# Odd layer's norm scale computed as columns and spread by a diagonal, and its first two input tiles multiplied side by side

## What is computed

```python
h_lat = rms_norm(x, norm_g[l]) * (1.0 + sc[:, None]) + sh[:, None]
h_ctx = rms_norm(ctx, norm_g[l]) * (1.0 + scc) + shc
# odd_mixer, pre(h), for context and column-ordered latents
xm, zg = jnp.split(h @ w_in, [ML_WIDTH], axis=-1)        # 2048 + 2048 columns
xcv = jax.nn.silu(centred_dwconv(xm, conv_w, conv_b))    # 4 taps along the tokens
# q, k, v and the gates g come from xcv and xm; zg gates the output
```

## Time and profile before

| | us |
|---|---|
| median of 3 runs | 3034.0 |
| the profiled execution | 3031.98 |
| its span, first to last instruction | 3030.3 |
| mean granted TensorE clock, share of full speed | 0.941 |
| DVE busy | 1542.8 |
| ACT busy | 843.1 |
| POOL busy | 1017.0 |

### The profile page before, as it was taken

One profiled execution on the slowest core, in us unless ns is written; L12 is line 12 of the kernel. 1 busy time (PEld: TensorE's weight loads), 2 busy tenths in 40 slices (PEclk: granted clock), 3 DMA queues, 4 the chain that ended last, 5 costly groups with the idle time before them and its releaser, 6 DMA issues.

```text
span 3030.3 us, 38093 instructions
## 1 busy us (share of the span) xinstructions
PE 2748.6 (91%) x13429; PEld 2132.5 (70%) x13429; DVE 1542.8 (51%) x2331; ACT 843.1 (28%) x1004; POOL 1017.0 (34%) x1181
## 2 busy tenths in 40 slices
PE   7994677998998999898996899998999999999898
PEld 5652665544444677887885677776788888888787
DVE  2204885487787322343324644577545555545711
ACT  1210454246256111322212322221323323231310
POOL 0000997788760000002123333343442423332000
PEclk8797888999999999899997999999999999999999
DMA  4520222010111666634113222245513131213521
GB/s 154 170 75 29 69 83 88 28 49 24 45 46 28 200 185 191 204 91 175 39 32 81 70 106 97 97 156 192 185 42 102 55 115 56 96 58 119 165 83 51
DMA packets 258720, 297.89 MB, mean 98 GB/s; under 512 B 34944, under 2 KB 222632, under 8 KB 258224
## 3 DMA queue, kind: packets, MB, share of 16 engines
q1 hardware_dynamic: 203104, 206.75, 21.6%
q10 hardware_dynamic: 50672, 72.89, 6.6%
q0 software_dynamic: 4832, 16.78, 1.9%
HBM read 203.09 MB, written 93.29 MB: 98 GB/s over the span
## 4 chain that ended last, share of the span: by engine, by line
PE 63%; DVE 10%; issue 4%; ACT 3%; POOL 1%; DMA 1%; DVEq 0%; SPq 0%; ACTq 0%; POOLq 0%
PE ps L130 55%; PE ps L1175 5%; PE ps L1024 1%; PE ps L1018 1%; DVE s_scan_tmp L1910 1%; DVE arena L1912 1%; DVE s_scan_tmp L1908 1%; DVE arena L485 1%; DVE xc_part L2204 1%; DVE arena L1961 0%; ACT arena L1337 0%; POOL h_part L2542 0%; ACT L1337 0%; DVE arena L1930 0%; PE ps L1180 0%
## 5 line engine op out<-in xcount | busy, mean ns | idle before, releaser
L130 PE MATMUL ps<-arena,weights 128*128 128x512 f32 (+2 forms) x2432 | 752.4, 488 | 52.4 <-ACT arena L1337 19.7
L130 PEld LDWEIGHTS ps<-arena,weights 128*128 128x128 f32 (+1 forms) x2432 | 398.5, 177 | 396.8 <-issue 325.0
L130 PE MATMUL ps<-h_part,in_weight_parts 128*128 128x512 f32 (+1 forms) x1920 | 420.6, 380 | 37.7 <-POOL in_weight_parts L2534 13.6
L130 PEld LDWEIGHTS ps<-h_part,in_weight_parts 128*128 128x128 f32 x1920 | 343.3, 192 | 110.5 <-POOL in_weight_parts L2534 14.3
L130 PE MATMUL ps<-v_part,p_part 128*128 128x512 f32 x1248 | 295.0, 395 | 0.1
L130 PEld LDWEIGHTS ps<-v_part,p_part 128*128 128x128 f32 x1248 | 234.2, 190 | 49.2 <-issue 0.9
L130 PE MATMUL ps<-q_part,xc_part 128*128 128x256 f32 x1920 | 249.0, 289 | 14.7 <-DVE v_part L2204 10.7
L130 PEld LDWEIGHTS ps<-q_part,xc_part 128*128 128x128 f32 x1920 | 238.5, 195 | 16.4 <-DVE v_part L2204 11.5
L1175 PE MATMUL ps<-wo_part,mx_part 128*128 128x512 f32 x768 | 183.8, 400 | 6.8 <-DVE mx_part L2204 6.2
L2531 POOL TENSOR_TENSOR in_weight_parts<-weights,ones 128x1024 fp32r<-128x1024 f32 x32 | 79.5, 2483 | 306.5 <-issue 213.7
L1175 PEld LDWEIGHTS ps<-wo_part,mx_part 128*128 128x128 f32 x768 | 145.6, 191 | 41.0 <-issue 6.4
(11 more groups left out here) (354 smaller groups left out, 4180.6 us busy)
## 6 DMA issues: line engine op xcount, KB each, us to landing
weights<-in_e_w_in SPq DMA_DIRECT2D x32, 512.0 KB, 4.2
weights<-in_o_w_in SPq DMA_DIRECT2D x32, 512.0 KB, 4.2
s_out_maps<-arena ACTq DMA_DIRECT2D x16, 640.0 KB, 2.9
weights<-in_mod_w POOLq DMA_DIRECT2D x20, 512.0 KB, 4.8
arena<-s_out_maps SPq DMA_DIRECT2D x16, 640.0 KB, 4.3
ml_xcv<-arena ACTq DMA_DIRECT2D x16, 640.0 KB, 3.0
xc_full<-ml_xcv SPq DMA_DIRECT2D x4, 2560.0 KB, 9.7
xm_tiles<-ml_xm SPq DMA_DIRECT2D x16, 640.0 KB, 3.9
```

Of the source, the lines that this page charges most:

```text
L130: return nc.tensor.matmul(o, lhsT, rhs, start=(k == 0), stop=(k == n - 1))
```

## The change

The sum over features is taken with the squares as weights and one column of ones as the moving side: ten products, one for each block of 128 tokens, leave the 1280 sums as ten columns of 128 partitions in bank 3. Root and reciprocal then work on 128 x 10. DVE multiplies the identity by these columns into ten diagonal blocks (diag, 128 x 1280), and PE multiplies them by ones: the scale of all tokens appears on all partitions, context in bank 6, latents in banks 4 and 5. ACT copies the context's scale to SBUF (rrow); DVE reads the latents' scale from PSUM. DVE makes all eight low parts; the unrounded copy h_full, ACT's second rounding and POOL's subtractions are gone. norm_tmp of k waits for the low part of k-2.

SP issues the first two weight loads ahead of the store of X2. PE runs tiles 0 and 1 together, k by k, into banks 0 to 2 and 3, 6, 7; ACT takes tile 0 out with two copies and tile 1 with four, one behind the other; the gate accumulation is opened after both. Then come tile 2, the sums of tiles 0 and 1, and the loop from tile 3. POOL's weight splits run one tile further ahead.

```diff
+        rsc, rrow = at(43584, NBLK), at(43600, CTX)
+        diag = at(43968, TOK).rearrange("p (b c) -> p b c", c=P)
+        psP = [[ps3[0][:, t0:t0 + n] for t0, n in SEGS], [ps[:, b, 0:n] for b, (t0, n) in zip((3, 6, 7), SEGS)]]
-        HL = over("h_full", DT * TOK, AR0 + 4 * XTo, F32)[:, :].rearrange("p (k t) -> p k t", k=DT)
...
             sp.wait_ge(*past("eo_wl", MT))
+            for s in range(2):
+                sp.dma_start(Wv[:, s], ow_in[s]).then_inc(sem(f"xz_w{s}"), 16)
             for s in range(2):
                 sp.wait_ge(*past(f"eo_ev{s}", 16))
             sp.dma_start(x2_d.rearrange("k p t -> p k t"), X2[:, :, CTX:TOK]).then_inc(sem("x_spilled"), 16)
...
-            with sp.Fori(0, MT // 2) as i:
+            with sp.Fori(1, MT // 2) as i:
                 for s in range(2):
                     input_weight(i, s)
...
             pe.wait_ge(*past("sq_total", 1))
-            for j, (t0, n) in enumerate(SEGS):
-                last = mm(ps[:, 4 + j, 0:n], ones[:, :], sq[1][:, 0, t0:t0 + n], 0, 1)
+            for b in range(NBLK):
+                last = mm(ps[:, 3, b:b + 1], sq[1][:, DT - 1, P * b:P * b + P], ones[:, 0:1], 0, 1)
             last.then_inc(sem("ss_mm1"), 1)
-            pe.wait_ge(*past("rms1", 3))
+            pe.wait_ge(*past("diag_ready", 1))
+            for b, (o, n) in ((0, (ps[:, 6, 0:CTX], 2)), (2, (ps[:, 4], 4)), (6, (ps[:, 5], 4))):
+                last = mm(o, ones[:, :], diag[:, b:b + n].rearrange("p b c -> p (b c)"), 0, 1)
+            last.then_inc(sem("scale_mm"), 1)
+            pe.wait_ge(*past("rms1", 1))
+            pe.wait_ge(*past("scale_row", 1))
+            for s in range(2):
+                pe.wait_ge(*past(f"xz_split{s}", 1))
+            for k in range(DT):
+                pe.wait_ge(*past("ht1_low", k + 1))
+                for s in range(2):
+                    for q, (a, b) in enumerate(PARTS):
+                        for j, (t0, n) in enumerate(SEGS):
+                            last = mm(psP[s][j], WXs[s][:, a, k], HTs[b][:, k, t0:t0 + n], 3 * k + q, 3 * DT)
+                    if k == DT - 1:
+                        last.then_inc(sem(f"xz_mm{s}"), 1)
+            pe.wait_ge(*past("xm_ev", 2))
             pe.wait_ge(*past("wf_zero", 1))
...
-            mixer_input(0, 0)
-            with pe.Fori(0, MT // 2 - 1) as i:
+            mixer_input(1, 0)
+            for s in range(2):
+                gate_sums(0, s)
+            with pe.Fori(1, MT // 2 - 1) as i:
                 mixer_input(i, 1)
                 gate_sums(i, 0)
                 mixer_input(i + 1, 0)
...
+                    nc.scalar.activation(rsc, ps[:, 3, 0:NBLK], ACT.Sqrt, bias=cols[:, 0:1], scale=1.0 / D).then_inc(sem("rms1"), 1)
+                    act.wait_ge(*past("scale_mm", 1))
+                    nc.scalar.activation(rrow, ps[:, 6, 0:CTX], ACT.Copy).then_inc(sem("scale_row"), 1)
...
-                    if l == 1 and k % 2:
-                        act.wait_ge(*past("ht1_full", k + 1))
-                        last = nc.scalar.activation(HTs[0][:, k], HL[:, k], ACT.Copy)
...
+            act.wait_ge(*past("xz_mm0", 1))
+            nc.scalar.activation(xmp[:, 0, 1:1 + CTX], psP[0][0][:, 0:CTX], ACT.Copy)
+            nc.scalar.activation(xmp[:, 0, LOFF + 1:LOFF + 1 + LAT], ps3[0][:, CTX:TOK], ACT.Copy).then_inc(sem("xm_ev"), 1)
+            act.wait_ge(*past("xz_mm1", 1))
+            nc.scalar.activation(xmp[:, 1, 1:1 + CTX], psP[1][0][:, 0:CTX], ACT.Copy)
+            x = LOFF + 1
+            for src in (psP[1][0][:, CTX:BANK], psP[1][1], psP[1][2]):
+                last = nc.scalar.activation(xmp[:, 1, x:x + src.shape[1]], src, ACT.Copy)
+                x += src.shape[1]
+            last.then_inc(sem("xm_ev"), 1)
+            for s in range(2):
+                mixer_rows(s, s)
+            with act.Fori(1, MT // 2) as i:
...
+                    link(V.reciprocal(rsc, rsc))
+                    V.tensor_tensor(diag, ident[:, :].unsqueeze(1).to_broadcast([P, NBLK, P]), rsc.unsqueeze(2).to_broadcast([P, NBLK, P]), ALU.mult).then_inc(sem("diag_ready"), 1)
+                    dve.wait_ge(*past("scale_mm", 1))
+                    dve.wait_ge(*past("scale_row", 1))
+                    scale = [psf[:, 4 * BANK:4 * BANK + LAT], rrow]
                 for k in range(DT):
...
-                    elif k >= 2 and k % 2:
-                        dve.wait_ge(*past("ht1_full", k - 1))
                     elif k >= 2:
-                        dve.wait_ge(*past("ht1_low", k // 2))
+                        dve.wait_ge(*past("ht1_low", k - 1))
...
-                    if l == 1 and k % 2:
+                    if l == 1 and k:
                         low_part(k - 1)
+                if l == 1:
+                    low_part(DT - 1)
...
                 input_weight(0, s)
-            for k in range(1, DT, 2):
-                pool.wait_ge(*past("ht1_high", k + 1))
-                pool.wait_ge(*past("bm", 3))
-                GP.tensor_tensor(HTs[1][:, k], HL[:, k], HTs[0][:, k].bitcast(F32), ALU.subtract).then_inc(sem("ht1_pool"), 1)
+            input_weight(1, 0)
             pool.wait_ge(*past("gates_open", 2))
             pool.wait_ge(*past("gates_mm", 1))
...
-                    input_weight(i + 1, s)
-            for m in range(2, MT):
+                    input_weight(i + (s + 1), 1 - s)
+            for m in range(3, MT):
                 input_weight((MT + m) // 2, m % 2)
```

More of the change, by code:

```diff
@@ L64 @@
 C_MCW = 256
-LATE_SIGNALS = ("sums", "ht1_full", "ht1_high", "ht1_low", "w_high", "xz_split0", "xz_split1", "xz_mm0", "xz_mm1",
+LATE_SIGNALS = ("sums", "scale_mm", "ht1_high", "ht1_low", "w_high", "xz_split0", "xz_split1", "xz_mm0", "xz_mm1",
     "xc_in", "xm_in0", "xm_in1", "xr_stored", "xb_in", "zt_in", "out_stored0", "out_stored1",
@@ L987, in mixer_input @@
                 for k in range(DT):
-                    if k % 2:
-                        pe.wait_ge(*past("ht1_pool", k // 2 + 1))
-                    else:
-                        pe.wait_ge(*past("ht1_low", k // 2 + 1))
                     for q, (a, b) in enumerate(PARTS):
@@ L1218, in norm @@
                 act.wait_ge(*past(f"ss_mm{l}", (DT, 1)[l]))
-                for j, (t0, n) in enumerate(SEGS):
-                    nc.scalar.activation(rstd[l][:, t0:t0 + n], ps[:, 4 + j, 0:n], ACT.Sqrt, bias=cols[:, 0:1], scale=1.0 / D).then_inc(sem(f"rms{l}"), 1)
+                if l == 0:
+                    for j, (t0, n) in enumerate(SEGS):
+                        nc.scalar.activation(rstd[0][:, t0:t0 + n], ps[:, 4 + j, 0:n], ACT.Sqrt, bias=cols[:, 0:1], scale=1.0 / D).then_inc(sem("rms0"), 1)
+                else:
+                    nc.scalar.activation(rsc, ps[:, 3, 0:NBLK], ACT.Sqrt, bias=cols[:, 0:1], scale=1.0 / D).then_inc(sem("rms1"), 1)
+                    act.wait_ge(*past("scale_mm", 1))
+                    nc.scalar.activation(rrow, ps[:, 6, 0:CTX], ACT.Copy).then_inc(sem("scale_row"), 1)
                 for k in range(DT):
@@ L1488, in _, with mixer_rows @@
             norm(1)
-            with act.Fori(0, MT // 2) as i:
+            def mixer_rows(m, s):
+                act.wait_ge(*past("mcv_ready", m + 1))
+                nc.scalar.activation(mcs, mcv, ACT.Sigmoid).then_inc(sem("mcs_ready"), 1)
+                act.wait_ge(*past("xm_ev", m + 1))
+                act.dma_start(xm_d[bass.ds(m, 1), :, 0:CTX].rearrange("o p t -> p (o t)"), xmp[:, s, 1:1 + CTX]).then_inc(sem(f"xm_stored{s}"), 16)
+                act.dma_start(xm_d[bass.ds(m, 1), :, CTX:TOK].rearrange("o p t -> p (o t)"), xmp[:, s, LOFF + 1:LOFF + 1 + LAT]).then_inc(sem(f"xm_stored{s}"), 16)
+                act.wait_ge(*past("xcv_ready", m + 1))
+                act.dma_start(xc_d[bass.ds(m, 1)].rearrange("o p t -> p (o t)"), xco[:, s]).then_inc(sem(f"xcv_stored{s}"), 16)
+            act.wait_ge(*past("xz_mm0", 1))
[11 more added lines that the diff above has]
+            with act.Fori(1, MT // 2) as i:
                 for s in range(2):
-                    m = 2 * i + s
                     act.wait_ge(*past(f"xz_mm{s}", i + 1))
@@ L1718, in norm @@
             def norm(l):
-                dve.wait_ge(*past(f"rms{l}", 3))
-                link(V.reciprocal(rstd[l], rstd[l]))
+                dve.wait_ge(*past(f"rms{l}", (3, 1)[l]))
                 if l == 0:
+                    link(V.reciprocal(rstd[0], rstd[0]))
                     modulation(0)
+                    scale = [rstd[0][:, CTX:TOK], rstd[0][:, 0:CTX]]
+                else:
+                    link(V.reciprocal(rsc, rsc))
[3 more added lines that the diff above has]
+                    scale = [psf[:, 4 * BANK:4 * BANK + LAT], rrow]
                 for k in range(DT):
@@ L2079, in _ @@
             dve.wait_ge(*past("sq_added", DT - 2))
[L2080 removed]
+            V.tensor_tensor(sq[1][:, DT - 1], sq[1][:, 0], sq[1][:, DT - 1], ALU.add).then_inc(sem("sq_total"), 1)
             dve.wait_ge(*past("eo_ev0", 16))
```

21 lines of the change are left out of this document (6 added, 15 removed).

## The result

The changed kernel takes 3014.6 us by the median of four runs (3013.0 to 3016.35), against 3034.4 of the kernel before beside them; the ratio is 0.9934, with an interval of 0.9917 to 0.9951, 15 to 25 us less. Measured again later, beside the experiments, it took 3016.8 us, ratio 0.9948 (0.9935 to 0.9962), 12 to 20 us less. It is faster, by little more than half a per cent; the forecast of 3012 was 2.6 to 4.8 us too low, and both medians lie inside its range.

What follows compares the result with a forecast made beforehand. TensorE was taken as the bound, so gains must come from its stalls around the odd layer's start: tile 3 starting at 1710.3 instead of 1732.47 gains 22.2 us, off the 3034.0 median giving 3012 us, range 3006 to 3020.

Steps and rivals of the forecast that it cites:

- The sum of squares: Odd layer's norm start: 20 column passes 4.5 us, root 0.3 for 1.63, reciprocal 0.2 with link for 8.15.
- The diagonal: VectorE's product over 1280 elements before the spreading: 2.3 us beside weight splits, bounds 1.5 to 3.9.
- The spreading: Three float32 products by ones over 1280 columns, 4.6 us at the low clock; norm_tmp then starts at 1646.9.
- The norm per k: VectorE makes all low parts: 3.45 us per k, no instruction stretched, PSUM read at no extra cost.
- The early weights: Loads ahead of the X2 store: GpSimd splits from 1633.7 to about 1643.8, eight us before TensorE wants them.
- The pair: Tiles 0 and 1 together: 18 matmuls at low clock, 7.15 us, then 126 in 24.6, ending at 1683.7.
- the lower bound: Clock rise in tiles 0 and 1 after one set of 9 matmuls, 1.8 us less than the forecast end.
- Covers that could fail here: Before tile 1's gate sums: VectorE's chain takes 10.8 or 11.5 us per tile, wait nothing or half a microsecond.
- The second rival: After tiles 0 and 1: table load, longer first convolution and gate sums waiting for VectorE, some 2 us; 3014; chance 0.12.
- The gain was not given back: After tile 3: rival that a queue that doesn't move keeps the end at 3034, citing a 5.63 us wait; 0.05.
- The norm did start earlier: Odd layer's norm: rival that slow passes and a delayed diagonal put first norm_tmp at 1650.8; 3016; chance 0.15.
- The clock did not stay low: Tiles 0 and 1: rival that the clock stays low, tile 3 starting 28 us late at 1760; 3062; chance 0.04.

Runs made afterwards that it cites:

- the run with the weights behind the store: Changed kernel with the first two weight loads put behind the store of X2 again; 3025.8 us, ratio to the kernel before 0.9979.
- the old scale: Changed kernel with the scale from three products by ones, three roots and a reciprocal over 1280 values, read from SBUF; 3020.7 us, ratio 0.9962.
- the tiles apart: Changed kernel with tile 0 multiplied whole before tile 1, same banks, weights and waits; 3017.1 us, ratio to the kernel before 0.9948.
- the splits moved: Changed kernel with GpSimd splitting weights for tiles 3 and 4 only after the product of tile 1; 3007.5 us, ratio to the kernel before 0.9913.
- the run with the fillers: Changed kernel with idle float32 matmuls (12, 8, 16, 24) into an unused bank in four TensorE pauses; 3014.1 us, ratio to the kernel before 0.9947.
- the fewer fillers: Changed kernel with splits after tile 1's product and idle matmuls, 10 instead of 16 and 22 instead of 24 in the last two pauses; 3003.4 us, 0.9908.
- the run with only the weights: Kernel before with only the first two weight loads moved ahead of the store of X2; 3024.1 us, ratio 0.9969.

## Why the prediction was right, and where it was not

**The sum of squares.** 20 passes in 4.40 us; forecast 4.5. The root took 0.27 us and the reciprocal 0.22, but from the end of the products to the diagonal, hand-overs included, it was 1.05 us (1637.07 to 1638.12) for the 0.6 of the forecast. The diagonal took 2.68 us for the 2.3 taken, inside its bounds, with split halves beside it all the time. In the run with the weights behind the store, where no split runs, the same instruction took 1.49. The spreading took 4.30 us (forecast 4.6). The first norm_tmp came 13.0 us after the mark; forecast 12.5.

**The norm per k.** 3.30 us (1650.57 to 1653.87 and so on), forecast 3.45, no instruction stretched, PSUM as fast as SBUF.

**The early weights.** Splits from 1632.0 to 1643.0, from 0.7 us before the mark to 10.3 behind it; the forecast had them from 0.7 before it to 9.4 behind it. What I did not work out is how much of the gain was theirs: 9.8 us alone, 10.5 when taken away. The forecast summed the new path and compared ends, which gives a total and hides the shares. As what the loads wait for it named the store, and not the gate row behind it.

**The pair.** 30.23 us instead of 31.75: the granted clock was 0.52 over 1653 to 1655 and 1.00 from there on, so it rose after some 4 us of work instead of 7.15, just above the lower bound (one set of 9, 3.57 us). The pair ended 48.2 us after the mark, forecast 49.3. Eviction 1.51 (1.45), opening 2.2 (2.15), tile 2 and the gate sums of tile 0 14.2 and 4.3: all right. Up to the end of the pair the forecast was 1.1 us too slow.

**The step that failed** is "Covers that could fail here": VectorE's chain per tile, 10.8 or 11.5 us, "nothing or half a microsecond" of waiting. It measured 15.8 us (1680.68 to 1696.49) and 12.7 (1696.75 to 1709.41), and the wait was 6.3 us. The rows were right for what they showed: one split, two GpSimd halves, beside the start of every convolution. In the changed kernel the first convolution has the splits of tiles 2 and 3 beside it, four halves, and the second those of tile 4. I had priced a stretched instruction for the diagonal, from the 3359 ns of the earlier trace rows, and not used it where the change moved three splits together. To this came a cost not in the sum: behind 6.3 us of idleness the gate sums began at the low clock (0.50 over 1709.5 to 1711.4, 0.51 to 1713.0, 1.00 then), 5.9 us for 4.3. Together -1.1 + 6.3 + 1.6 = 6.8 of the 7.2 us that the stretch fell short; the rest is that the forecast counted tile 3's start before by the chain (1732.47) and W counts it by TensorE (1732.12). The second rival named this wait at 2 us and a chance of 0.12, from three causes together: right in kind and a third of its size. Of its causes the stretched convolution was the one; the table load ahead of the first eviction did not come (ScalarE's copy at 1679.19 has none before it).

**Luck.** The median came nearer than the mechanism earns. With 15.0 us off the stretch and nothing else, it would have been 3019.4 beside the first runs of the kernel before and 3018.8 beside the later ones; 3014.6 and 3016.8 were measured. The other 4.8 and 2.0 us are in no part of the forecast, and no run shows a cause for them beyond the scatter between executions. The range of 3006 to 3020 would have held either way, but only just.

**Later.** The gain was not given back: the wait of the earlier trace rows is 5.6 us again, and the rest of the program is the same within its scatter.

**Rivals.** The norm did start earlier, by 1.9 us against the kernel before and the old scale. The clock did not stay low. The gain that the pairing promised TensorE was real, 7.5 us by the tiles apart, and was taken back in the next stage; with the splits moved it stays (74.6 against 82.0 us, where the tiles apart have no such wait to lose). That the late splits would do nothing for the tiles apart is argued from its unbroken TensorE rows and was not run.

## What to carry to other kernels

When a change brings two tiles together, everything that served them one by one comes together too: list what each other engine now does in that window, and price VectorE's two-input instructions beside GpSimd's by their stretched rows. A load issued behind other transfers can be the costliest thing in a stage, though its own row is short: read what was issued ahead of it, the small scattered row (23.3 us to landing for 4 KB) as well as the large store (12.8 us for 4096 KB). How near a median came to its forecast says little of the mechanism: compare the two on the stretch that was changed. And undo each part of a change by itself: here the columns and the diagonal gave 3 us, the pairing nothing until the splits were moved, and two moved DMA issues gave 10.

## What the runs showed of the hardware

Beside back-to-back GpSimd instructions that read SBUF, a VectorE pass of 1283 elements with two SBUF inputs took 3.40 to 3.73 us instead of 1.55, that is 1.9 to 2.2 us more, while the GpSimd halves beside it took 2.4 to 3.5 us. The first pass of the convolution, with one tensor input, was stretched too, less: 1.68 us beside a split (1680.68) and 0.95 without one (1696.75). An instruction with its second tensor input in PSUM was not touched: in the run with the weights behind the store, 1658.86 took 1.27 us wholly beside a split half (1658.73, 2.41 us), while its SBUF-only neighbours took 5.65, 2.44 and 2.57. The Trainium skill (SBUF — State Buffer, section "SBUF: two separate sides") says that the pair of ports shared by the two engines is held for a whole instruction and wanted by VectorE operations with two SBUF inputs; the rows of the instructions with two tensor inputs agree.

TensorE's granted clock could be held up with work that computes nothing. With fillers in TensorE's pauses it stayed at 1.00, the 2.4 GHz level, up to and through the column sums (1628.9 to 1637.7 in the run with the fillers); in the changed kernel, with pauses of 2.93 and 1.97 us there, it was at 0.50, the 1.2 GHz level, during these sums:

```profile
1632.60:1637.10 4.50, 4.40 (x20) 4.34 (x20) 0.00 (x0) 0.00 (x0) 4.42 (x2) 0.50 1.02 393
```

But pauses are not the whole of it. In the rows of the fewer fillers the clock is 1.00 over 1632.0 to 1634.2, with the twenty one-column passes, and 0.56 over 1634.2 to 1638.1, though the engine was busy for 2.20 of 2.20 and for 3.90 of 3.90 us. And in the run with only the weights the clock was 1.00 over 1640.8 to 1643.0, behind the same products and pauses to 0.1 us behind which it was 0.50 in the kernel before: the opening of the gate sums took 2.42 us in the one and 4.64 in the other. What made the clock fall or rise in these two places was not found.
